# VectorE makes the T sums of a Strassen FFN in pairs with slots of their own; product order, loads, gate row and last powers moved

## The reference

```
mod = silu(c) @ w_ada + b_ada          # sh1, s1, g1, shm, smx, gm, sh2, s2, g2
h = x + 0.5 * g1 * swiglu(rms(x) * (1 + s1) + sh1)      # hidden width 2816
z = (rms(h) * (1 + smx) + shm) @ w_in                    # conv GLU | q latent | kv latent | rope key
a = silu(layernorm(depthwise_conv31(glu(z)) + conv_b))
q, k = rms over each head (8 heads of 96), gains, rope;  att = softmax(q k / sqrt(96)) v
h = h + gm * (concat[a, att] @ w_out)
h = h + 0.5 * g2 * swiglu(rms(h) * (1 + s2) + sh2)
out = rms(h) * g_final
```

## Time and profile before

| | us |
|---|---|
| median of the runs | 2053.18 (2052.6 to 2054.25) |
| profiled execution | 2050.71 |
| its span in the trace | 2048.7 |
| TensorE busy | 1923.5 |
| VectorE busy | 1406.4 |
| GpSimd busy | 816.2 |
| ScalarE busy | 703.1 |

### The profile page before, as it was taken

How to read it: one execution, slowest core, us unless ns; L and a number is a source line. 1 busy time by engine, 2 the same in 40 slices (tenths; PEclk the granted TensorE clock), 3 DMA queues, 4 the chain that set the end, 5 groups by cost and what they waited for, 6 DMA issues and landing times.

```text
span 2048.7 us, 22259 instructions
## 1 busy us (share of the span) xinstructions
PE 1923.5 (94%) x8298; PEld 1524.9 (74%) x8298; DVE 1406.4 (69%) x1697; ACT 703.1 (34%) x1006; POOL 816.2 (40%) x590
## 2 busy tenths in 40 slices
...
DMA packets 95928, 196.43 MB, mean 96 GB/s; under 512 B 5453, under 2 KB 58804, under 8 KB 92755
## 3 DMA queue, kind: packets, MB, share of 16 engines
...
...
## 4 chain that ended last, share of the span: by engine, by line
PE 65%; DVE 14%; issue 8%; POOL 6%; DMA 5%; ACT 2%; SPq 0%; DVEq 0%; POOLq 0%; ACTq 0%
PE ps L499 23%; PE ps L580 22%; PE ps L389 7%; PE ps L2087 4%; DMA ada_raw<-in_w_ada 3%; PE ps L1100 2%; POOL sums L459 2%; PE ps L1078 2%; PE ps L1998 2%; DVE cv L1253 2%; DVE negmax L1037 2%; POOL HID L562 2%; DVE B L712 1%; DVE T L663 1%; POOL rqk L1181 1%
## 5 line engine op out<-in xcount | busy, mean ns | idle before, releaser
L499 PE MATMUL ps<-T,ring 128*128 128x512 f32 x1920 | 444.7, 391 | 0.0
L499 PEld LDWEIGHTS ps<-T,ring 128*128 128x128 f32 x1920 | 360.4, 188 | 77.9 <-issue 3.4
L499 PE MATMUL ps<-B,ring 128*128 128x512 f32 x1440 | 339.0, 392 | 0.0
L593 DVE TENSOR_TENSOR H<-ps,H 128x512 f32<-128x512 f32 x352 | 238.7, 687 | 123.6 <-PE ps L580 123.2
L499 PEld LDWEIGHTS ps<-B,ring 128*128 128x128 f32 x1440 | 270.9, 188 | 60.3 <-issue 3.2
L580 PE MATMUL ps<-WD,AT 128*128 128x512 f32 x1152 | 265.9, 390 | 9.8 <-issue 6.0
L580 PEld LDWEIGHTS ps<-WD,AT 128*128 128x128 f32 x1152 | 215.0, 188 | 56.7 <-issue 6.8
L336 POOL TENSOR_TENSOR rawd<-rawd,grow 128x1024 f32<-128x1024 f32 x44 | 104.7, 2402 | 352.1 <-DMA rawd<-in_ffn_wd 352.1
L562 POOL TENSOR_TENSOR HID<-HID,SG 128x512 f32<-128x512 f32 x80 | 130.5, 1635 | 236.5 <-DVE HID L548 115.1
L580 PE MATMUL ps<-WDL,AT 128*128 128x512 f32 x960 | 219.8, 389 | 0.0
L580 PEld LDWEIGHTS ps<-WDL,AT 128*128 128x128 f32 x960 | 179.9, 188 | 38.3 <-DVE H L593 1.0
...
## 6 DMA issues: line engine op xcount, KB each, us to landing
ada_raw<-in_w_ada SPq DMA_DIRECT2D x56, 512.0 KB, 3.9
hr<-ffn_hidden SPq DMA_DIRECT2D x22, 1024.0 KB, 6.8
rawd<-in_ffn_wd SPq DMA_DIRECT2D x22, 1024.0 KB, 4.9
rawg<-in_ffn_wg SPq DMA_DIRECT2D x21, 1024.0 KB, 6.0
rawu<-in_ffn_wu SPq DMA_DIRECT2D x21, 1024.0 KB, 5.2
...
H<-in_x SPq DMA_DIRECT2D x16, 512.0 KB, 7.1
ada<-in_w_ada SPq DMA_DIRECT2D x8, 1024.0 KB, 14.3
```

What stands on the lines that cost most here:

```text
L499: mm = e.matmul(ps[:, product_bank(M, k)], ring[:, place % RING, wx, kc], RIGHT[k][:, xx, kc], start=(kc == 0 and i == 0), stop=(kc == HC ...
L593: e.tensor_tensor(dst, ps[:, 4 + q % DB], dst, ALU.add).then_inc(f.added.sem, 1)
```

## The change

The T differences move from GpSimd to VectorE (`dve_t`). Pairs 2 and 3 get slots of their own, `late`, which overlay `rawu` while group 0 runs; `act_modulate` waits for no T form any more. VectorE cuts all eight units first, then makes pairs 0 and 1, then 2 and 3. The order of the seven products becomes P1, P2, P3, P6, P7, P5, P4, so that the three on B stand first, with C12 made together with C22 and W and C21 last. SP loads group 1's up weights only after all T forms are cut; in the last group it asks for the down weights before the hidden rows. The gate row of the second FFN moves from turn 2 to turn 3. In the head stage the last two tiles' powers are raised for head 0 alone at first, the other heads' after the first slots; tile 7's `vn` copy and rotation come later.

```diff
     [("hr0", [P, CPG, S], F32), ("hr1", [P, CPG, S], F32), ("sums", [P, 4, HALF], F32)],
+    [("_g4", [P, KC, GW], F32), ("late", [P, 4, HALF], F32)],
...
-K_P1, K_P2, K_P6, K_P7, K_P5, K_P4, K_P3 = range(PRODUCTS_OF)
-RIGHT = (B11, B21, T2, T3, T1, T4, B22)
+K_P1, K_P2, K_P3, K_P6, K_P7, K_P5, K_P4 = range(PRODUCTS_OF)
+RIGHT = (B11, B21, B22, T2, T3, T1, T4)
...
-OUTS = ("C11", "U2", "V", "C22", "W", "C21", "C12")
-QUARTERS = ("C11", "C22", "C21", "C12")
+OUTS = ("C11", "U2", "V", "C22", "W", "C12", "C21")
+QUARTERS = ("C11", "C22", "C12", "C21")
...
-    return {K_P1: (quadrant(M, 0, 0), 0), K_P6: (summed(1), 2), K_P7: (summed(2), 3), K_P5: (summed(0), 1),
-            K_P2: (quadrant(M, 0, 1), 0), K_P4: (quadrant(M, 1, 1), 0), K_P3: (summed(3), 4)}[k]
+    return {K_P1: (quadrant(M, 0, 0), 0), K_P2: (quadrant(M, 0, 1), 0), K_P3: (summed(2), 3), K_P6: (summed(1), 2),
+            K_P7: (summed(3), 4), K_P5: (summed(0), 1), K_P4: (quadrant(M, 1, 1), 0)}[k]
...
-    e.wait_ge(t_lo, n.t_forms + 4 * HC)
...
+    e.wait_ge(t_lo, n.t_forms + 2 * HC)
     done = (M - FIRST_M) * 4
     for s, (a, b, op, need, freed) in enumerate(((a21, a22, ALU.add, 0, K_P5), (summed(0), a11, ALU.subtract, 1, K_P6),
-                                                 (a11, a21, ALU.subtract, 0, K_P7),
-                                                 (a12, summed(1), ALU.subtract, 2, K_P3))):
+                                                 (a12, summed(1), ALU.subtract, 2, K_P3),
+                                                 (a11, a21, ALU.subtract, 0, K_P7))):
...
+        elif k == K_P3:
+            e.wait_ge(*f.mul(4))
         elif k == K_P6:
-            e.wait_ge(*f.mul(4))
             e.wait_ge(t_lo, n.t_forms + 4 * HC)
...
     elif what == "C21":
+        e.wait_ge(*f.w_out(out_made(M, "V")))
         ins = e.tensor_tensor(to[:, Q21], bank(K_P4), to[:, Q21], ALU.add)
...
-            e.wait_ge(*f.w_out(out_made(LAST_M, ("W", "C21", "C12")[q])))
+            e.wait_ge(*f.w_out(out_made(LAST_M, ("V", "W", "C21")[q])))
...
 def t_source(p):
-    x12, x22 = sums[:, 2 * (p % 2)], sums[:, 2 * (p % 2) + 1]
-    return base[:, p], x12, x22, base[:, HC + p]
-
-def pool_t(e, n, p):
+    x = (sums, late)[p // 2]
+    return base[:, p], x[:, 2 * (p % 2)], x[:, 2 * (p % 2) + 1], base[:, HC + p]
+def dve_t(e, n, p):
     b11, x12, x22, b21 = t_source(p)
     done = n.t_forms + 4 * p
-    if p == 0:
-        e.wait_ge(x_lo, n.units + KC)
-    e.wait_ge(modulated, n.units + KC + 2 * p + 1)
     e.tensor_tensor(b11, x12, b11, ALU.subtract).then_inc(t_add, 1)
-    e.wait_ge(x_lo, n.units + KC + 2 * p + 2)
...
-    if n.forms and h == 1 and i >= 4:
-        e.wait_ge(t_lo, n.t_forms + 4 * (i // 2 - 1))
...
-def sp_ffn(e, f, w, rows):
-
-    sp_load_gu(e, f, w, 1)
+def sp_ffn(e, f, w, rows, t_done):
+    e.wait_ge(*f.gu_lo(2 * CPG))
+    e.dma_start(rawg[:], w[0][:, :, GW:2 * GW]).then_inc(f.g_in.sem, 16)
...
     if f is fs[0]:
         e.wait_ge(*f.gu_mm(4))
         e.dma_start(grow[:], A["b_ada"][:, G1 * D:(G1 + 1) * D].broadcast_to([P, D])).then_inc(g1_in, 16)
+    e.wait_ge(t_lo, t_done)
+    e.dma_start(rawu[:], w[1][:, :, GW:2 * GW]).then_inc(f.u_in.sem, 16)
...
-                sp_load_hidden(e, f, m)
                 if m == 1:
                     sp_load_d(e, f, w, 0)
+                sp_load_hidden(e, f, m)
...
-    for s in (1, 2):
-        act_silu(e, f, s)
-    for k in range(RING // 2):
-        act_left_hi(e, f, FIRST_M, k)
+    act_silu(e, f, 1)
+    act_hi_t(e, n, 0)
+    act_hi_t(e, n, 1)
+    act_silu(e, f, 2)
+    act_left_hi(e, f, FIRST_M, K_P1)
+    act_left_hi(e, f, FIRST_M, K_P2)
+    act_hi_t(e, n, 2)
+    act_left_hi(e, f, FIRST_M, K_P3)
     act_silu(e, f, 3)
-    for k in range(RING // 2, PRODUCTS_OF):
+    act_hi_t(e, n, 3)
+    for k in range(K_P6, PRODUCTS_OF):
         act_left_hi(e, f, FIRST_M, k)
...
+    dve_hidden(e, f, 0)
+    dve_cut_x(e, n, range(KC, 2 * KC))
+    dve_hidden(e, f, 1)
+    for p in (0, 1):
+        dve_t(e, n, p)
+    for p in (0, 1):
+        dve_lo_t(e, n, p)
     dve_hidden(e, f, 2)
-    for k in range(RING // 2):
-        dve_left_lo(e, f, FIRST_M, k)
+    dve_left_lo(e, f, FIRST_M, K_P1)
+    dve_left_lo(e, f, FIRST_M, K_P2)
+    for p in (2, 3):
+        dve_t(e, n, p)
+    dve_left_lo(e, f, FIRST_M, K_P3)
     dve_hidden(e, f, 3)
-    for k in range(RING // 2, PRODUCTS_OF):
+    for p in (2, 3):
+        dve_lo_t(e, n, p)
+    for k in range(K_P6, PRODUCTS_OF):
         dve_left_lo(e, f, FIRST_M, k)
...
-            if f is fs[1] and M == FIRST_M:
+            if f is fs[1] and M == FIRST_M + 1:
                 if k == 0:
-                    e.wait_ge(*f.gu_mm(4))
                     dve_row_diag(e, G2)
-                elif k == 1:
+                elif k == 2:
                     dve_row_copy(e, 1)
                     e.wait_ge(row_ok, 4)
                     dve_half_row(e, f)
             if k == 0 and M > FIRST_M:
-                dve_out(e, f, M - 1, "C12")
-            for what in ((), (), ("C11",), ("U2",), ("V",), ("C22", "W"), ("C21",))[k]:
+                dve_out(e, f, M - 1, "C21")
+            for what in ((), (), ("C11",), (), ("U2",), ("V",), ("C22", "W", "C12"))[k]:
...
-    for p in range(HC):
-        pool_t(e, n, p)
     pool_sums(e, f, n, FIRST_M)
...
-            if f is fs[1] and M == FIRST_M and k == 0:
+            if f is fs[1] and M == FIRST_M + 1 and k == 1:
+                e.wait_ge(*f.w_out(out_made(FIRST_M, "V")))
                 pe_row(e, 1)
...
-def pool_inv_rms(e, t):
...
+def pool_inv_rms(e, t, heads=(0, NHD)):
     e.wait_ge(qk_sum, t + 1)
     e.tensor_scalar(qs[:, t], qs[:, t], 1.0 / QK, EPS, ALU.mult, ALU.add).then_inc(qk_mean, 1)
     e.wait_ge(qk_mean, t + 1)
-    e.tensor_tensor(rqk[:, t], qs[:, t], mhalf[:], ALU.pow).then_inc(qk_rstd, 1)
+    r, ms, power = (of_heads(x, slice(t, t + 1), *heads)
+                    for x in (rqk, qs, mhalf[:].unsqueeze(1).broadcast_to([P, NT, 2 * NHD])))
+    e.tensor_tensor(r, ms, power, ALU.pow).then_inc(qk_rstd, 1)
+def pool_late_inv_rms(e):
+    for t in range(LATE, NT):
+        r, ms, power = (of_heads(x, slice(t, t + 1), 1, NHD)
+                        for x in (rqk, qs, mhalf[:].unsqueeze(1).broadcast_to([P, NT, 2 * NHD])))
+        e.tensor_tensor(r, ms, power, ALU.pow).then_inc(qk_rstd, 1)
+    e.wait_ge(qk_rstd, 2 * NT - LATE)
...
+            pool_inv_rms(e, t, (0, 1) if t >= LATE else (0, NHD))
...
     pool_first_slots(e)
+    pool_late_inv_rms(e)
     pool_slots(e, 0, 1)
...
+    def half_free():
+        act_silu(e, f, 0)
+        e.wait_ge(*f.gu_lo(2 * CPG))
     act_norm(e, n, SH1, S1, lambda t: e.wait_ge(x_in[t], 16), first_weights, lambda: act_hi_gu(e, f, 0, 1, None),
-             lambda: act_silu(e, f, 0))
-    act_hi_t(e, n, HC - 1)
+             half_free)
...
-        e.wait_ge(up_out, 2 * t + 2)
+        e.activation(kn[:, t], kv[:, :, 0:NOPE], ACT.Copy, scale=zstat[:, 5 * NT + t:5 * NT + t + 1]).then_inc(kn_out, 1)
+        if t < NT - 1:
+            e.activation(vn[:, t], kv[:, :, NOPE:NOPE + VH], ACT.Copy, scale=zstat[:, 5 * NT + t:5 * NT + t + 1])\
+                .then_inc(up_out, 1)
+        e.wait_ge(up_out, 2 * t + 1)
+        e.wait_ge(kn_out, t + 1)
...
-
+        if t == NT - 1:
+            e.activation(vn[:, t], kv[:, :, NOPE:NOPE + VH], ACT.Copy, scale=zstat[:, 5 * NT + t:5 * NT + t + 1])\
+                .then_inc(up_out, 1)
...
-        rotate_q(t, 0)
         sl = sq[:, t % 2]
+        if t < NT - 1:
+            rotate_q(t, 0)
         e.tensor_reduce(qs[:, t, 0:NHD], sl[:, 0:NHD * QK].rearrange("p (h d) -> p h d", d=QK), AX_X, ALU.add)
-        rotate_q(t, 1)
+        rotate_q(t, 1 if t < NT - 1 else 0)
...
-        rotate_q(t, 2)
+        if t < NT - 1:
+            rotate_q(t, 2)
...
+    rotate_q(NT - 1, 1)
+    rotate_q(NT - 1, 2)
```

More of the change, by code:

```diff
@@ L153, in build @@
         CZ = (czh, czl)
-        rawg, rawu, rawd, hr0, hr1, sums, vec, wqr, _u2, latb, _g3, _u3, wkv, slot, qs, _s2, att, wor = region(
+        rawg, rawu, rawd, hr0, hr1, sums, _g4, late, vec, wqr, _u2, latb, _g3, _u3, wkv, slot, qs, _s2, att, wor = region(
             24 * KB, [("rawg", [P, KC, GW], F32), ("rawu", [P, KC, GW], F32), ("rawd", [P, CPG, D], F32)],
             [("hr0", [P, CPG, S], F32), ("hr1", [P, CPG, S], F32), ("sums", [P, 4, HALF], F32)],
+            [("_g4", [P, KC, GW], F32), ("late", [P, 4, HALF], F32)],
             [("vec", [NV, P], F32)],
@@ L285, in build @@
         up_scaled, up_hi, up_lo, up_mm, up_out = (sem(n) for n in ("up_scaled", "up_hi", "up_lo", "up_mm", "up_out"))
-        qk_sq, qk_sum_t, qk_sum, qk_mean, qk_rstd, rope = (sem(n) for n in (
-            "qk_sq", "qk_sum_t", "qk_sum", "qk_mean", "qk_rstd", "rope"))
+        qk_sq, kn_out, qk_sum_t, qk_sum, qk_mean, qk_rstd, rope = (sem(n) for n in (
+            "qk_sq", "kn_out", "qk_sum_t", "qk_sum", "qk_mean", "qk_rstd", "rope"))
```

(30 more changed lines are left out.)

23 lines of the change are left out of this document (4 added, 19 removed).

## The result

| | before | changed |
|---|---|---|
| median of the runs on one chip, us | 2052.89 (2052.17 to 2054.25) | 2023.16 (2022.4 to 2025.55) |
| profiled execution, us | 2050.71 | 2023.33 |
| its span | 2048.7 | 2021.5 |

The ratio of the times is 0.9861, with a 95% interval of 0.9848 to 0.9873. The forecast was 2023.2. The medians are 29.7 apart, the two profiled executions 27.4; what follows divides the spans' difference, 27.2.

What follows compares the result with a forecast made beforehand. TensorE, busy 1923.5 of 2048.7 us, was taken as the bound. Gains of 8.9 (first FFN), 15.1 (second FFN) and 6.0 (head stage) sum to 30.0 us, giving 2023.2 us against the median 2053.18; range 2011 to 2033.

Steps and rivals of the forecast that it cites:

- The pass change: First transposes to product P1: TensorE's two stops and slow clock go, 16.1 us in the first FFN, 16.4 in the second.
- The rival that VectorE's difference stays at 1.7 without GpSimd: VectorE's T differences stay slow, each FFN loses some 20 us net: near 2058 us; chance 0.02.
- P6's wait of 0.9: First group of each FFN: TensorE waits about 0.9 us before P6, as `t_lo` is full at 8.4 after P1's start.
- The stop at turn 3, 4.0: First FFN, M=3: P3 waits for C12, late from up weights and column pieces; TensorE stops 4.0 us.
- The clock behind this stop, 2.3: First FFN, matmuls after the wait for C12: slow clock costs 2.3 us, bounds 0.1 and 3.
- The gate row, 4.2: Second FFN, M=3: TensorE stops 4.2 us for the gate row in place of 3.77, at the same price in clock.
- rival A: VectorE catches up and no stop stands at the second turn: 2009 us; chance 0.16.
- B: Rival: VectorE is later, both stops 3 us longer and P6's wait 2: gain 19 to 22, 2032 us; chance 0.22.
- E: Rival: the FFN part moves the stop to P6 whole, only the head's 6 and some is left: 2045 us; chance 0.04.
- The ends, 0 with -1 to +1: End of each FFN's products: later P6 and P7 and the earlier down load cost 0, bounds -1 to +1 us per FFN.
- The head, 6.0 with 4.5 to 6.5: Head stage: tile 7's power for head 0 ends at 931.5 instead of 937.5, gaining 6.0 us, bounds 4.5 to 6.5.
- rival C: The new order makes TensorE wait for C12 in every turn, at P3 of 38 turns: 2076 us; chance 0.04.

Runs made afterwards that it cites:

- the run with GpSimd's differences: The changed kernel with the 16 T differences made by GpSimd again, slots of their own and product order kept: 2030.88 us, ratio to before 0.9894.
- the head-only trace: The kernel before with only the head stage's part of the change: 2048.94 us, ratio to before 0.9984.

## Why the prediction was right, and where it was off

**The pass change**: right in both FFNs to 0.1. The rival that VectorE's difference stays at 1.7 without GpSimd is refuted (0.61 to 0.73 start to start; the two beside GpSimd's sums took 1.77 and 1.67, as expected), and the run with GpSimd's differences shows what the move itself brings.

**P6's wait of 0.9**: 0. `t_lo` was full 7.5 after P1's start, not 8.4, and P6's left cut was made at 8.1, just before P6 was due at 8.2. The chain had the very links of the prediction; rounded durations summed to 0.9 too much, 0.2 of it in the adding up (its terms give 8.2).

**The stop at turn 3, 4.0**: the place, the cause (late up weights and pieces) and the customer (C12) right, the size 2.59. C12 was made 27.2 after P1's start, not 29.3, and P3 was due at 24.8, not 25.4, which leaves 1.4 less. Of the 2.1 by which C12 was sooner, 0.9 is `t_lo`'s, but that took P6's wait of 0.9 away too and so shortened the stop little; 0.5 lies between `t_lo` and turn 3's cut for P6 (done at 19.7, not 21.1), and 0.7 behind it, where the third piece's load was there in time. The up weights landed 5.0 after they were asked for. The 4.4 that the prediction sets beside its 5.2 comes from a fit that the Trainium skill, DMA: Bandwidth & Descriptors, Anatomy of one DMA, gives for DMAs on GpSimd's path; this load is issued by SP. The clock behind this stop, 2.3: 1.7. Not predicted: the g1 row's stop of 0.98 behind it. Together -4.96 for -7.2.

**The gate row, 4.2**: 4.98; the row, VectorE's diagonal beside GpSimd (2.28) and the place were right. So rival A, no stop at the second turn, is out in both FFNs; the gain of B, 19 to 22, and E's 2045 are out by the time.

**The ends, 0 with -1 to +1**: the step "VectorE's last two weight cuts still end the 3.06 stop", at no cost, was right for its length. It missed that with the earlier load the stop would have been 1.47 but for the new order. And it put the clock at nothing: in the second FFN the clock fell behind the stop, -1.54 between these two traces, outside its bound. That is the clock's scatter as much as the change: with the FFNs of before the clock fell there too in the head-only trace (group 24.36), and in two of the six traces with the new end the group took 23.9.

**The head, 6.0 with 4.5 to 6.5**: 4.67. The failed step is "Its power ends at 931.5 in place of 934.61 + 2.90 = 937.5", taken whole as 6.0. The power did end 5.9 sooner, but TensorE waits for the slot operations behind it, and the sum carried them over at their old length. Two of them were moved beside another engine's work. Of the rule cited there, the Trainium skill's SBUF — State Buffer, Who interferes with whom, only the half on two SBUF inputs was used; the same section says that copy, cast and tensor_scalar of VectorE can take the shared ports too, where their operands allow it. By it these two slot operations had to be looked at beside the two ones rows, and the traces agree (1.39 and 1.81 beside them, 0.41 and 0.84 without).

**Order, settled turns**: 19.04 unchanged, as predicted; rival C (a wait for C12 in every turn) is refuted.
